# Feed-forward up projection with seven half-block products in place of eight, and its weights' low halves all made on VectorE

## The chip, the cores and the metric

The kernel runs on one core of one Trainium2 chip. The metric is the device time of one execution in microseconds. The kernel before takes 1625.59 us (median of 3 runs, 1625.49 to 1627.17).

## What is computed

Three blocks run one after another on a sequence of 512 tokens with 1024 features, in float32: a gated attention block, a gated retention block, and a mixer block (long convolution and gated linear attention) that ends in a feed-forward network. The change lies in that feed-forward network alone, which is the last stage before the final norm:

```python
def _sq_relu_mlp(h, w1, w2):
    return jnp.square(jax.nn.relu(h @ w1)) @ w2

        h2 = _rms_norm(x, norm_mlp[l]) * (1.0 + sc2) + sh2
        x = x + g2 * _sq_relu_mlp(h2, w_mlp1[l], w_mlp2[l])
    ...
    return _rms_norm(x, norm_final)
```

`h2` is 512 x 1024, `w1` 1024 x 4096, `w2` 4096 x 1024.

## The kernel before

Activations lie with features on the partitions: `X`, `HH` and `HL` are 128 x 8 x 512 (eight groups of 128 features, 512 tokens). Every float32 product is made from two halves: a value is split into a high half (rounded to fp32r) and a low half (the rest), and three matmuls are summed in PSUM: high x high, low x high, high x low. `HH` and `HL` are the high and low halves of the normed input, `FHI` and `FLO` those of the squared hidden activations.

Weights come as a stream of 246 tiles of 128 x 1024 values (512 KB), in the order of `PLAN`. Each tile is 512 input features by 256 output features. It is loaded into one of five `raw` buffers, ScalarE copies its high half into one of three `wh` buffers, and VectorE or GpSimd (the set `DVE_LOW` says which) subtracts to get the low half into one of three `wl` buffers. The class `Feed` sets where in each engine's program this is done: whenever an engine's code takes tile u, it first issues the work that it has on the tiles up to u + 2. Each engine works its program strictly in the order in which the code was written, so an instruction that waits holds up everything behind it.

An "up" unit u (0 to 15) makes 256 of the 4096 hidden features: two weight tiles, 48 matmuls of 512 columns (2 tiles x 2 output groups x 4 input groups x 3), in banks 0 and 1. Then ScalarE applies the relu out of PSUM, VectorE squares, ScalarE makes `FHI` (128 x 512), and VectorE or GpSimd makes `FLO`. A "down" unit takes a tile of `w2` in two output groups of 128 (nt = 0 in bank 0, nt = 1 in bank 1), with eight matmuls on the high half of the tile and four on the low half for each group; VectorE then adds the bank, scaled, to `X`. In the code `done("kept", tag, j)` is the mark that the bank j of a unit has been read, `free[b]` is what TensorE waits for before it starts a new sum in bank b, and `done("w free", u)` is the mark that TensorE has read tile u. Before the change the order is: up units in groups of four, then the four down units of the group before, each of these of two tiles (1024 hidden features).

TensorE instructions carry line 427 (all matmuls), ScalarE copies line 1972 (`copy`), other ScalarE work line 1969, VectorE's scalar_tensor_tensor line 1130. Both engines' code of the feed-forward part is in the functions `up` and `down`.

Of the kernel before, what the change touches and what calls it, by code (L numbers as in the profile page):

```python
# [19 lines left out]
T = 512  # L20
# [18 lines left out]

def weight_plan():  # L40
# [71 lines left out]
    down(3)
# [5 lines left out]
DVE_LOW = frozenset([*range(73), 164])  # L118
# [131 lines left out]
def build(nc, a, out, stack):  # L250
# [172 lines left out]
    def tensor(pe):  # L423
# [653 lines left out]
        unit_f(("up", 0, 0), (0, 1), *hi_lo("x3"), hooks=[nothing, first_scale, nothing, nothing])  # L1077

        def up(g):
            for n in range(4):  # L1080
                u = 4 * g + n
                if u:
                    unit_f(("up", g, n), (2, 3) if u == 1 else (0, 1), *hi_lo("x4"), by_k=2 if u == 1 else 0)

        def down(g):
            for n in range(4):
                for kh in range(2):
                    u = feed.take()
                    pe.wait_ge(*(done("l", "f", g, k) for k in range(4 * kh, 4 * kh + 4)))
                    features(("down", g, n), FHI[g % 2], FLO[g % 2], range(4 * kh, 4 * kh + 4), kh == 0, kh == 1, (0, 1), u,  # L1090
                             kh=kh)
# [31 lines left out]
    def vector(dve):  # L1123
# [18 lines left out]
        def split(i, u):  # L1142
            if u in DVE_LOW:
# [3 lines left out]
                by_dve.also("raw free", i)  # L1147

# [1827 lines left out]
```

## Time and profile before

| | |
|---|---|
| median of 3 runs | 1625.59 us |
| the profiled execution | 1626.04 us |
| its span | 1624.3 us |
| TensorE busy | 1607.9 us (99%) |
| TensorE weight load busy | 1336.6 us (82%) |
| VectorE busy | 829.1 us (51%) |
| ScalarE busy | 680.8 us (42%) |
| GpSimd busy | 583.0 us (36%) |
| DMA, mean | 110 GB/s |

Span is the time from the first to the last instruction in the trace; 1.7 us of the execution lie around it. Matmuls are pipelined, so the busy time of one matmul is longer than the distance from its start to the next one's start; the distance is what a matmul costs in a dense stretch.

### The profile page before, as it was taken

Reading aid. Unit: us, or ns where it says so; the run is one execution under the profiler, and the core shown is the slowest. Engines: PE = TensorE matmul, PEld = TensorE weight load, DVE = VectorE, ACT = ScalarE, POOL = GpSimd, SP = SyncE. Lnnn points to the kernel's source line nnn. Section 1 sums busy time; section 2 is a strip of 40 time slices with the busy share of each in tenths; the row PEclk is TensorE's granted clock in tenths of the full one; section 3 lists DMA queues with packets and bytes.
Section 4 is the critical chain, followed back from the end, with each engine's and each line's share of the span. In section 5 each row is a group of like instructions: output and inputs, shape, how many; then the busy total and the mean of one; then the engine's idle time right before and its main releaser. Section 6 shows DMA issues by size and latency. Waiting matters only on the chain.

```text
span 1624.3 us, 20270 instructions
## 1 busy us (share of the span) xinstructions
PE 1607.9 (99%) x8308; PEld 1336.6 (82%) x8308; DVE 829.1 (51%) x1239; ACT 680.8 (42%) x1043; POOL 583.0 (36%) x289
## 2 busy tenths in 40 slices
PE   9999999999999999999999999999999999999998
PEld 6888898889888878888887767789878788888887
DVE  7787867676665364443443646681356621111112
ACT  6533343443432433555455463423435643332323
POOL 1002113221344434334333434353323465555542
PEclk9999999999999999999999999999999999999999
DMA  6453333343355223233223241122112133222221
GB/s 234 153 204 131 125 127 134 116 132 121 133 205 207 104 91 104 93 103 103 94 90 121 78 156 66 52 87 73 53 40 78 65 117 104 91 103 92 98 85 52
DMA packets 53252, 179.16 MB, mean 110 GB/s; under 512 B 6428, under 2 KB 7068, under 8 KB 52776
## 3 DMA queue, kind: packets, MB, share of 16 engines
q1 hardware_dynamic: 53160, 177.88, 31.5%
q8 instruction: 65, 1.06, 0.3%
q14 instruction: 27, 0.22, 0.0%
HBM read 172.58 MB, written 2.12 MB: 108 GB/s over the span
## 4 chain that ended last, share of the span: by engine, by line
PE 92%; DVE 5%; ACT 1%; issue 1%; DMA 0%; SPq 0%; POOL 0%; DVEq 0%; ACTq 0%; POOLq 0%
PE banks L427 90%; PE banks L430 2%; DVE ACC L1182 1%; DVE wl L1146 1%; ACT T L1969 0%; DMA maskf<-cst_dram 0%; DVE ada L1130 0%; DVE X L1130 0%; ACT wh L1972 0%; ACT Sc L1969 0%; DVE ML L1130 0%; DVE T L1912 0%; ACT L1969 0%; DVE Sc L1130 0%; DVE E L1912 0%
## 5 line engine op out<-in xcount | busy, mean ns | idle before, releaser
L2553 POOL TENSOR_TENSOR wl<-raw,wh 128x1024 fp32r<-128x1024 f32 x171 | 424.2, 2485 | 525.3 <-ACT wh L1972 525.3
L427 PE MATMUL banks<-HH,wh 128*128 128x512 f32 (+1 forms) x1040 | 413.2, 397 | 2.6 <-ACT T L1969 0.9
L427 PE MATMUL banks<-HL,wh 128*128 128x512 f32 (+1 forms) x1040 | 402.3, 390 | 0.3 <-DVE HL L1130 0.3
L1972 ACT ACTIVATE wh<-raw 128x1024 fp32r<-128x1024 f32 x246 | 257.0, 1052 | 296.9 <-PE banks L427 289.0
L427 PE MATMUL banks<-HH,wl 128*128 128x512 f32 x1032 | 282.6, 390 | 0.0
L427 PEld LDWEIGHTS banks<-HH,wh 128*128 128x128 f32 (+1 forms) x1040 | 194.9, 187 | 50.0 <-issue 5.5
L427 PEld LDWEIGHTS banks<-HL,wh 128*128 128x128 f32 (+1 forms) x1040 | 194.7, 187 | 42.0 <-issue 1.4
L427 PEld LDWEIGHTS banks<-HH,wl 128*128 128x128 f32 x1032 | 193.4, 188 | 41.5 <-issue 1.0
L427 PE MATMUL banks<-wh,HH 128*128 128x256 f32 x448 | 128.5, 287 | 0.0
L427 PE MATMUL banks<-wl,HH 128*128 128x256 f32 x448 | 126.7, 283 | 0.0
L427 PE MATMUL banks<-wh,HL 128*128 128x256 f32 x448 | 126.6, 283 | 0.0
L1146 DVE TENSOR_TENSOR wl<-raw,wh 128x1024 fp32r<-128x1024 f32 x74 | 89.5, 1231 | 28.3 <-ACT wh L1972 28.3
L427 PE MATMUL banks<-OH,wh 128*128 128x512 f32 x256 | 103.1, 403 | 0.3 <-issue 0.3
L1130 DVE SCALAR_TENSOR_TENSOR X<-banks,mod,X 128x512 f32<-128x512 f32 (+1 forms) x41 | 30.1, 736 | 142.3 <-PE banks L427 142.3
L427 PE MATMUL banks<-OL,wh 128*128 128x512 f32 x256 | 99.8, 390 | 0.0
L427 PE MATMUL banks<-FHI,wh 128*128 128x512 f32 x256 | 99.6, 389 | 0.0
L427 PE MATMUL banks<-FLO,wh 128*128 128x512 f32 x256 | 99.6, 389 | 0.0
L2562 POOL TENSOR_TENSOR OL<-T,OH 128x512 fp32r<-128x512 f32 x21 | 28.3, 1349 | 197.4 <-ACT OH L1972 197.4
L1912 DVE TENSOR_TENSOR T<-T 128x512 f32<-128x512 f32 x30 | 28.3, 942 | 113.9 <-ACT T L1969 113.8
L427 PEld LDWEIGHTS banks<-wh,HL 128*128 128x128 f32 x448 | 85.7, 191 | 0.5 <-issue 0.2
L427 PEld LDWEIGHTS banks<-wh,HH 128*128 128x128 f32 x448 | 85.7, 191 | 0.5 <-issue 0.2
L427 PEld LDWEIGHTS banks<-wl,HH 128*128 128x128 f32 x448 | 85.7, 191 | 0.0
(354 smaller groups left out, 2627.5 us busy)
## 6 DMA issues: line engine op xcount, KB each, us to landing
raw<-wst_dram SPq DMA_DIRECT2D x294, 512.0 KB, 3.2
X<-xT_dram SPq DMA_DIRECT2D x8, 512.0 KB, 6.6
CB<-sums_dram SPq DMA_DIRECT2D x12, 256.0 KB, 3.1
D<-dec_dram SPq DMA_DIRECT2D x12, 256.0 KB, 2.8
out_dram<-XT SPq DMA_DIRECT2D x8, 256.0 KB
QS<-QX SPq DMA_DIRECT2D x24, 64.0 KB, 2.6
KSw<-KX SPq DMA_DIRECT2D x24, 64.0 KB, 2.0
MX<-memT_dram SPq DMA_DIRECT2D x2, 512.0 KB, 8.7
```

Of the source, the lines that this page charges most:

```text
L427: return pe.eng.matmul(dst, w, x, start=start, stop=stop, skip_group_check=True)
L430: return pe.eng.transpose(dst, x, ident[:, :])
L1130: return eng.scalar_tensor_tensor(out=dst, in0=x, scalar=s, in1=y, op0=op0, op1=op1)
L1146: tt(wl[:, q, :], raw[:, i % NRAW, :], wh[:, q, :].bitcast(F32), ALU.subtract).then_inc(*by_dve("low", u))
L1182: i = tt(acc[:, 0:n], acc[:, 0:n], q[:, 0:n], ALU.add)
L1912: tt(t[:, :], t[:, :], t[:, :], ALU.mult).then_inc(*by_dve("f", g, k))
L1972: return eng.activation(dst, src, ACT.Copy)
L2553: tt(wl[:, q, :], raw[:, i % NRAW, :], wh[:, q, :].bitcast(F32), ALU.subtract).then_inc(*by_pool("low", u))
L2562: tt(OL[:, tile, :], t[:, :], OH[:, tile, :].bitcast(F32), ALU.subtract).then_inc(*by_pool("l", "o", l, tile))
```

## The change

The up units 4 to 15 are computed by the Winograd form of Strassen's product. The weight tile is a 2 x 2 arrangement of blocks (256 input features by 128 output features each), the input a 2 x 2 arrangement (256 features by 256 tokens), and the product is made of seven block products in place of eight. Per tile these are seven products of 2 x 3 matmuls of 256 columns, 84 in a unit of two tiles, in banks 2 to 5. In place of each plain block some products take sums of blocks:

- of the weights: four sums per tile (`WS`), made on VectorE by three instructions (512, 256 and 256 elements), split by ScalarE (`SH`) and VectorE (`SL`)
- of the input: four sums per half (`XS`), made once in the units 2 and 3 on VectorE from `XW`, the whole values, which GpSimd adds from `HH` and `HL`; their halves are `XSH` and `XSL`
- of the products: ScalarE copies the first (`PS`), VectorE adds the others up by four instructions, and then makes relu and square in one instruction.

The order of the units changes too: each up unit from 2 on is followed by two down units of one tile each (512 hidden features), so that `FHI` and `FLO` hold half as many features and `X` is updated 64 times in place of 32. The set `DVE_LOW` now holds the tiles 192 to 245, so GpSimd makes no weights' low halves there (the tiles 190 and 191 are its last). GpSimd makes all `FLO` from unit 4 on.

```diff
+FF = [("up", 0), ("up", 1)]
+for _g in range(1, 8):
+    for _h in range(2):
+        FF += [("up", 2 * _g + _h), ("down", _g - 1, 2 * _h), ("down", _g - 1, 2 * _h + 1)]
+FF += [("down", 7, _n) for _n in range(4)]
...
+SEVEN = 4
...
+    for step in FF:
+        if step[0] == "up":
+            pair("up", 0, 8, (256 * step[1],), "s" if step[1] >= SEVEN else "w")
+        else:
+            pair("down", 4 * step[1], 4 * step[1] + 4, (256 * step[2],))
...
-DVE_LOW = frozenset([*range(73), 164])
+S_TILES = [u for u, w in enumerate(w for w in PLAN if w[0] != "ada") if w[0] == "s"]
+S_AT = {u: v for v, u in enumerate(S_TILES)}
+NS = 3
+DVE_LOW = frozenset([*range(73), 164, *range(192, 246)])
...
+        def seven(u):
+            for kh in range(2):
+                w = feed.take()
+                high, low = blocks(wh[:, w % NW, :]), blocks(wl[:, w % NW, :])
+                sums = [s[:, S_AT[w] % NS, :].rearrange("p (s q c) -> p s q c", s=4, q=2) for s in (SH_, SL_)]
+                def of_w(j, i):
+                    return high[:, j, :, i, :], low[:, j, :, i, :]
+                def of_s(n):
+                    return sums[0][:, n, :, :], sums[1][:, n, :, :]
+                def of_x(j, h):
+                    return [x[:, 4 * kh + 2 * j:4 * kh + 2 * j + 2, 256 * h:256 * h + 256] for x in (HH, HL)]
+                def of_t(n):
+                    return XSH[:, kh, n, :, :], XSL[:, kh, n, :, :]
+                def product(b, c, a, x):
+                    o, s0 = bank[b][:, 256 * c:256 * c + 256], kh == 0 and c == 0
+                    for q in range(2):
+                        mm(o, a[0][:, q, :], x[0][:, q, :], s0 and q == 0, False)
+                        mm(o, a[0][:, q, :], x[1][:, q, :], False, False)
+                    for q in range(2):
+                        i = mm(o, a[1][:, q, :], x[0][:, q, :], False, kh == 1 and q == 1)
+                    return i
+                pe.wait_ge(done("high", w), done("low", w), done("x sums", kh), *free[2])
+                product(2, 0, of_w(1, 0), of_x(1, 0))
+                product(2, 1, of_w(0, 0), of_x(0, 0)).then_inc(*by_pe("seven", u, kh, 0))
+                pe.wait_ge(done("sums high", w), done("sums low", w), *free[3])
+                product(3, 0, of_w(1, 1), of_t(3))
+                product(3, 1, of_s(2), of_t(1)).then_inc(*by_pe("seven", u, kh, 1))
+                pe.wait_ge(*free[4])
+                product(4, 0, of_s(1), of_t(0))
+                product(4, 1, of_s(0), of_t(2)).then_inc(*by_pe("seven", u, kh, 2))
+                pe.wait_ge(*free[5])
+                product(5, 0, of_s(3), of_x(1, 1)).then_inc(*by_pe("seven", u, kh, 3))
+                by_pe.also("w free", w)
...
+            for b in range(2, 6):
+                free[b] = tuple(done("kept", ("up", u), j) for j in range(2))
...
+        def down(g, n):
+            u = feed.take()
+            pe.wait_ge(*(done("l", "f", g, k) for k in range(4)))
+            features(("down", g, n), FHI[g % 2], FLO[g % 2], range(4), True, True, (0, 1), u)
...
+            if PLAN[i][0] == "s":
+                v = S_AT[u]
+                w, s = blocks(raw[:, i % NRAW, :]), WS[:, v % 2, :].rearrange("p (s q c) -> p s q c", s=4, q=2)
+                dve.wait_ge(done("raw", i), done("sums low", S_TILES[v - 2]) if v > 1 else done("l", "f", 0, 1))
+                tt(s[:, 0:2, :, :], w[:, 0, :, :, :].rearrange("p q i c -> p i q c"), w[:, :, :, 1, :],
+                   ALU.subtract).then_inc(*by_dve())
+                dve.wait_ge(by_dve.last())
+                tt(s[:, 2, :, :], w[:, 1, :, 1, :], s[:, 0, :, :], ALU.add).then_inc(*by_dve())
+                dve.wait_ge(by_dve.last())
+                tt(s[:, 3, :, :], w[:, 1, :, 0, :], s[:, 2, :, :], ALU.subtract).then_inc(*by_dve("summed", i))
+                dve.wait_ge(done("sums high", u))
+                tt(SL_[:, v % NS, :], WS[:, v % 2, :], SH_[:, v % NS, :].bitcast(F32), ALU.subtract).then_inc(*by_dve("sums low", u))
...
+        def x_sums(kh):
+            x = XW[:, 4 * kh:4 * kh + 4, :].rearrange("p (j q) (h c) -> p j q h c", q=2, c=256)
+            b11, b12, b21, b22 = (x[:, j, :, h, :] for j in range(2) for h in range(2))
+            dve.wait_ge(*(done("x whole", k) for k in range(4 * kh, 4 * kh + 4)), done("l", "f", 0, 1),
+                        done("x sums", kh - 1) if kh else None)
+            tt(XS[0][:, 0, :, :], b12, b11, ALU.subtract).then_inc(*by_dve())
+            stt(XS[1][:, 0, :, :], b22, -1.0, b12, ALU.mult, ALU.subtract).then_inc(*by_dve())
+            dve.wait_ge(by_dve.last())
+            tt(XS[0][:, 1, :, :], b22, XS[0][:, 0, :, :], ALU.add).then_inc(*by_dve("x summed", kh, 0))
+            dve.wait_ge(by_dve.last())
+            tt(XS[1][:, 1, :, :], b21, XS[0][:, 1, :, :], ALU.subtract).then_inc(*by_dve("x summed", kh, 1))
...
+        def seven(u):
+            g, n = u // 2, 2 * (u % 2)
+            kept = done("kept", ("up", u - 1), 0) if u > SEVEN else None
+            dve.wait_ge(done("seven", u, 1, 1), done("first product", u), kept)
+            tt(PS[:, 1, :], bank[3][:, 256:512], PS[:, 0, :], ALU.add).then_inc(*by_dve())
+            dve.wait_ge(done("seven", u, 1, 2), by_dve.last())
+            tt(PS[:, 2:4, :], psum[:, 4, :].rearrange("p (a c) -> p a c", a=2), PS[:, 1:2, :].to_broadcast([128, 2, 256]),
+               ALU.add).then_inc(*by_dve())
+            t = turn("hidden", g, n + 1)
+            dve.wait_ge(by_dve.last(), temp_free("hidden", g, n + 1))
+            tt(t[:, :].rearrange("p (a c) -> p a c", a=2), psum[:, 3:5, 0:256], PS[:, 3:4, :].to_broadcast([128, 2, 256]),
+               ALU.add).then_inc(*by_dve("kept", ("up", u), 1))
+            hidden(g, n + 1, t)
+            t = turn("hidden", g, n)
+            dve.wait_ge(done("seven", u, 1, 3), temp_free("hidden", g, n))
+            tt(t[:, :].rearrange("p (a c) -> p a c", a=2), psum[:, 2:6:3, 0:256], PS[:, 0:3:2, :],
+               ALU.add).then_inc(*by_dve("kept", ("up", u), 0))
+            hidden(g, n, t)
+        def hidden(g, k, t):
+            dve.wait_ge(by_dve.last())
+            stt(t[:, :], t[:, :], 0.0, t[:, :], ALU.max, ALU.mult).then_inc(*by_dve("f", g, k))
...
+            if u == 2:
+                x_sums(0)
+            if u == 3:
+                x_sums_low(1)
...
+        def down(g, n):
+            feed.take()
+            for j in range(2):
+                t = 2 * n + j
+                dve.wait_ge(done("unit", ("down", g, n), j), done("kept", ("down", g - 1, n), j) if g else None)
...
+                stt(X[:, t, :], bank[j], mod[:, 40 + t:41 + t], X[:, t, :], ALU.mult, ALU.add).then_inc(*by_dve("kept", ("down", g, n), j))
...
+            if (g, n) == (0, 0):
+                x_sums_low(0)
+            if (g, n) == (0, 1):
+                x_sums(1)
...
+            if PLAN[i][0] == "s":
+                v = S_AT[u]
+                act.wait_ge(done("summed", i), done("w free", S_TILES[v - NS]) if v >= NS else None)
+                copy(SH_[:, v % NS, :], WS[:, v % 2, :]).then_inc(*by_act("sums high", u))
...
+            if u >= SEVEN:
+                act.wait_ge(done("seven", u, 1, 0), done("kept", ("up", u - 1), 0) if u > SEVEN else done("x sums", 1))
+                copy(PS[:, 0, :], bank[2][:, 256:512]).then_inc(*by_act("first product", u))
+                for k in (2 * (u % 2) + 1, 2 * (u % 2)):
+                    high(g, k, temp("hidden", g, k))
...
-            if made[0] % 3:
+            if made[0] % 3 or g >= SEVEN // 2:
...
+        def x_whole(k):
+            pool.wait_ge(done("h", "x4", k), done("l", "x4", k))
+            tt(XW[:, k, :], HH[:, k, :].bitcast(F32), HL[:, k, :].bitcast(F32), ALU.add).then_inc(*by_pool("x whole", k))
...
+            for k in (1, 0) if u >= SEVEN else (0, 1):
+                k += 2 * (u % 2)
+                if low(g, k, temp("hidden", g, k)):
+                    by_pool.also("temp", turns["hidden", g, k])
+            if u == 1:
+                for j in range(2):
+                    low(g, j, E[j])
+            if u in (1, 2):
+                for k in range(4 * u - 4, 4 * u):
+                    x_whole(k)
```

VectorE, from the down units that stand before the up unit 4 on; a row "wl<-raw,wh" is the low half of a weight tile, "T<-T" is a square. Before, all of VectorE's work between the hidden features of two groups:

```order
L1912 TENSOR_TENSOR T_84<-T_84 128x512 [waits scalar_done]
L1130 SCALAR_TENSOR_TENSOR X<-banks,mod,X 128x512 [waits tensor_done] x8
L1912 TENSOR_TENSOR T_84<-T_84 128x512 [waits scalar_done]
L1912 TENSOR_TENSOR T_85<-T_85 128x512 [waits scalar_done]
L1916 TENSOR_TENSOR FLO_207<-T_85,FHI_205 128x512 [waits scalar_done]
```

And now, behind the low halves of the two down tiles that follow an up unit, to the first of these two tiles' update of `X`:

```order
L2010 TENSOR_TENSOR PS<-banks,PS 128x256 [waits scalar_done,tensor_done]
L2012 TENSOR_TENSOR PS<-banks,PS 128x512 [waits vector_done,tensor_done]
L2016 TENSOR_TENSOR T_84<-banks,PS 128x512 [waits gpsimd_done,vector_done]
L1186 SCALAR_TENSOR_TENSOR T_84<-T_84 128x512 [waits vector_done]
L2021 TENSOR_TENSOR T_85<-banks,PS 128x512 [waits gpsimd_done,tensor_done]
L1186 SCALAR_TENSOR_TENSOR T_85<-T_85 128x512 [waits vector_done]
L1202 TENSOR_TENSOR wl<-raw,wh 128x1024 [waits scalar_done]
L1208 TENSOR_TENSOR WS<-raw 128x512 [waits raw_in1]
L1211 TENSOR_TENSOR WS<-raw,WS 128x256 [waits vector_done]
L1213 TENSOR_TENSOR WS<-raw,WS 128x256 [waits vector_done]
L1215 TENSOR_TENSOR SL<-WS,SH 128x1024 [waits scalar_done]
L1186 SCALAR_TENSOR_TENSOR X<-banks,mod,X 128x512 [waits tensor_done] x2
```

Six instructions on the products and five on the next up unit's first tile now stand ahead of the update of `X` by the first down tile; nothing stood ahead of the eight updates before.

ScalarE at the same place, now (a row "wh<-raw" is the high half of a tile; the third of them is that of the next up unit's first tile):

```order
L2088 ACTIVATE wh<-raw 128x1024 [waits tensor_done,raw_in4]
L2088 ACTIVATE wh<-raw 128x1024 [waits tensor_done,raw_in0]
L2088 ACTIVATE PS<-banks 128x256 [waits tensor_done]
L2088 ACTIVATE FHI_214<-T_84 128x512 [waits vector_done]
L2088 ACTIVATE FHI_214<-T_85 128x512 [waits vector_done]
L2088 ACTIVATE wh<-raw 128x1024 [waits tensor_done,raw_in1]
L2088 ACTIVATE SH<-WS 128x1024 [waits vector_done]
```

The high half of the next up unit's first tile stands behind the two `FHI` of the unit before, which wait for VectorE.

TensorE, at the boundary between the two down tiles behind such an up unit, now (the last matmuls of the first tile, and the first of the second, which starts a new sum in bank 0):

```order
L445 MATMUL banks<-FHI_214,wh 128x512
L445 MATMUL banks<-FLO_216,wh 128x512
L445 MATMUL banks<-FHI_214,wl 128x512 x4
L445 MATMUL banks<-FHI_214,wh 128x512 [waits vector_done,scalar_done]
L445 MATMUL banks<-FLO_216,wh 128x512
```

The wait for `vector_done` is that for the first down tile's update of `X` out of bank 0 (`free[0]`).

GpSimd around the units 1 and 2, before:

```order
L2685 TENSOR_TENSOR FLO_207<-T_85,FHI_205 128x512 [waits vector_done,scalar_done]
L2685 TENSOR_TENSOR FLO_207<-E_204,FHI_205 128x512 [waits vector_done,scalar_done]
L2553 TENSOR_TENSOR wl<-raw,wh 128x1024 [waits scalar_done] x2
L2685 TENSOR_TENSOR FLO_207<-T_84,FHI_205 128x512 [waits vector_done,scalar_done]
L2553 TENSOR_TENSOR wl<-raw,wh 128x1024 [waits scalar_done] x2
```

And now:

```order
L2815 TENSOR_TENSOR FLO_216<-E_204,FHI_214 128x512 [waits vector_done,scalar_done]
L2820 TENSOR_TENSOR XW<-HH,HL 128x512 x4
L2683 TENSOR_TENSOR wl<-raw,wh 128x1024 [waits scalar_done] x2
L2815 TENSOR_TENSOR FLO_217<-T_84,FHI_215 128x512 [waits vector_done,scalar_done]
L2820 TENSOR_TENSOR XW<-HH,HL 128x512 x4
L2683 TENSOR_TENSOR wl<-raw,wh 128x1024 [waits scalar_done] x2
```

Four additions `XW` stand ahead of the low halves of the tiles 188 and 189, and four more ahead of those of 190 and 191.

## Rows read from the trace of the kernel before

**Rows 1.** The page: busy time by engine, and the chain that ended last

```profile
PE 1607.9 (99%) x8308; PEld 1336.6 (82%) x8308; DVE 829.1 (51%) x1239; ACT 680.8 (42%) x1043; POOL 583.0 (36%) x289
PE 92%; DVE 5%; ACT 1%; issue 1%; DMA 0%; SPq 0%; POOL 0%; DVEq 0%; ACTq 0%; POOLq 0%
```

**Rows 2.** Windows: the start, and the feed-forward stage from unit 3 on

```profile
0.00:8.00 8.00, 6.75 (x19) 2.54 (x19) 2.06 (x5) 3.68 (x4) 0.20 (x4) 1.00 0.76 250
1297.50:1614.00 316.50, 316.50 (x1399) 261.95 (x1399) 59.93 (x76) 101.35 (x127) 162.76 (x77) 1.00 0.25 88
```

**Rows 3.** Timeline of TensorE: matmuls of 512 columns, 12 from 1371.32 to 1374.04

```profile
1371.32 0.39 PE L427 MATMUL banks<-FHI,wh 128*128 128x512 f32 x1
...
1374.04 0.39 PE L427 MATMUL banks<-FHI,wh 128*128 128x512 f32 x1
```

**Rows 4.** Timeline of TensorE: matmuls of 256 columns, 55 from 269.87 to 276.47

```profile
269.87 0.28 PE L427 MATMUL banks<-wh,HH 128*128 128x256 f32 x1
...
276.47 0.28 PE L427 MATMUL banks<-wh,HL 128*128 128x256 f32 x1
```

**Rows 5.** Timelines of VectorE and ScalarE: what TensorE's progress releases

```profile
1371.52 0.75 DVE L1130 SCALAR_TENSOR_TENSOR X<-banks,mod,X 128x512 f32<-128x512 f32 x1 [7.41 <-PE banks L427]
...
1374.30 1.06 ACT L1972 ACTIVATE wh<-raw 128x1024 fp32r<-128x1024 f32 x1 [4.38 <-PE banks L427]
```

**Rows 6.** Groups by shape: durations on ScalarE, VectorE and GpSimd

```profile
L1972 ACT ACTIVATE FHI<-T 128x512 fp32r<-128x512 f32 x30 | 19.0, 633 | 30.3 <-DVE T L1912 30.3
L1969 ACT ACTIVATE T<-banks 128x512 f32<-128x512 f32 x35 | 20.8, 595 | 44.8 <-PE banks L427 44.7
L1904 DVE TENSOR_TENSOR E<-banks,R 128x512 f32<-128x512 f32 x2 | 1.3, 680 | 0.0
L1368 DVE TENSOR_TENSOR PL<-banks,PH 128x256 fp32r<-128x256 f32 x12 | 5.0, 413 | 0.0
L1130 DVE SCALAR_TENSOR_TENSOR HL<-X,gx,HH 128x512 fp32r<-128x512 f32 x8 | 6.0, 747 | 1.5 <-ACT HH L1969 1.5
L1146 DVE TENSOR_TENSOR wl<-raw,wh x74: 1208/1217/1714, 6.3 to 1074.2; 128x1024 fp32r<-128x1024 f32 x74
L1916 DVE TENSOR_TENSOR FLO<-T,FHI x9: 692/692/1007, 1302.8 to 1517.7; 128x512 fp32r<-128x512 f32 x9
```

**Rows 7.** The chain, in order of time: from VectorE's end to TensorE's start

```profile
1196.17 0.77 DVE KEC L1760 x2
1196.94 0.14 issue
1197.08 0.94 PE banks L427 x3
```

**Rows 8.** Timelines of GpSimd and VectorE around 1301 to 1311 us

```profile
1301.47 1.75 POOL L2685 TENSOR_TENSOR FLO<-T,FHI 128x512 fp32r<-128x512 f32 x1
1303.75 4.75 POOL L2553 TENSOR_TENSOR wl<-raw,wh 128x1024 fp32r<-128x1024 f32 x2 [0.54 <-ACT wh L1972]
1309.79 1.29 POOL L2685 TENSOR_TENSOR FLO<-T,FHI 128x512 fp32r<-128x512 f32 x1 [1.29 <-ACT FHI L1972]
...
1300.43 1.63 DVE L1912 TENSOR_TENSOR T<-T 128x512 f32<-128x512 f32 x1 [1.18 <-ACT T L1969]
...
1306.87 2.18 DVE L1912 TENSOR_TENSOR T<-T 128x512 f32<-128x512 f32 x1 [3.11 <-ACT T L1969]
1310.23 1.40 DVE L1912 TENSOR_TENSOR T<-T 128x512 f32<-128x512 f32 x1 [1.18 <-ACT T L1969]
```

**Rows 9.** Timelines of GpSimd and TensorE around the end of unit 2

```profile
1295.06 1.30 POOL L2685 TENSOR_TENSOR FLO<-E,FHI 128x512 fp32r<-128x512 f32 x1 [1.89 <-ACT FHI L1972]
1296.31 5.21 POOL L2553 TENSOR_TENSOR wl<-raw,wh 128x1024 fp32r<-128x1024 f32 x2
...
1297.51 0.47 PE L427 MATMUL banks<-HH,wh 128*128 128x512 f32 x1 [0.94 <-ACT T L1969]
```

**Rows 10.** TensorE: its first matmuls, and its longest waits in the whole trace

```profile
1.25 7.03 PE L427 MATMUL banks<-Z 128*128 128x512 bf16 x18 [1.25 <-DVE Z L1263]
PE banks L427 <- DVE wl L1146: 2.3, 4, 1.0
```

More of the change, by code:

```diff
@@ L1075, in first_scale @@
             free[6] = (done("sum kept", "x3"),)
[L1077 to L1091, printed above, removed]
@@ L1894, in norm_half @@
             for k in ks:
-                dve.wait_ge(done("scale rows", "x3"), done("l", "x4", k - 2) if k > 1 else None, *(done("half", ("up", 0, 0), kh, j) for j in range(2)))
+                dve.wait_ge(done("scale rows", "x3"), done("l", "x4", k - 2) if k > 1 else None, *(done("half", ("up", 0), kh, j) for j in range(2)))
                 stt(bank[4 + k % 2], X[:, k, :], gx2[:, k:k + 1], bank[7], ALU.mult, ALU.mult).then_inc(*by_dve("x4", k))
@@ new lines, in x_sums_low @@
+        def x_sums_low(kh):
+            for n in range(2):
+                dve.wait_ge(done("x sums high", kh, n), done("x summed", kh, 1))
+                tt(XSL[:, kh, 2 * n:2 * n + 2, :, :], XS[n][:, :, :, :], XSH[:, kh, 2 * n:2 * n + 2, :, :].bitcast(F32),
+                   ALU.subtract).then_inc(*by_dve("x sums", kh))
+        def seven(u):
[16 more added lines that the diff above has]
+            hidden(g, n, t)
@@ new lines, in down @@
+        def down(g, n):
[3 more added lines that the diff above has]
+                dve.wait_ge(done("unit", ("down", g, n), j), done("kept", ("down", g - 1, n), j) if g else None)
+                if g == 7 and t == 7:
+                    for h in range(2):
+                        c = slice(256 * h, 256 * h + 256)
+                        stt(X[:, t, c], bank[j][:, c], mod[:, 40 + t:41 + t], X[:, t, c], ALU.mult, ALU.add).then_inc(*by_dve("last tile", h))
+                    by_dve.also("kept", ("down", g, n), j)
+                    turn("last", "x5")
+                    continue
+                stt(X[:, t, :], bank[j], mod[:, 40 + t:41 + t], X[:, t, :], ALU.mult, ALU.add).then_inc(*by_dve("kept", ("down", g, n), j))
+                if g == 7:
+                    add_square("x5", t, T, t == 0, t == 6, free=done("sum", "x3"))
+            if (g, n) == (0, 0):
+                x_sums_low(0)
+            if (g, n) == (0, 1):
+                x_sums(1)
@@ L1955, in vector @@
+        for step in FF[1:]:
+            (up if step[0] == "up" else down)(*step[1:])
         dve.wait_ge(done("root"))
@@ new lines, in down @@
+        def down(g, n):
+            if (g, n) == (7, 0):
+                fn(sm[:, 0:1], one, ACT.Sqrt).then_inc(*by_act())
+            feed.take()
+            for j in range(2):
+                t, m = 2 * n + j, done("kept", ("down", g, n), j)
+                if g == 7 and t == 7:
+                    q = temp("last", "x5")
+                    act.wait_ge(temp_free("last", "x5"))
+                    for h in range(2):
+                        c = slice(256 * h, 256 * h + 256)
+                        act.wait_ge(done("last tile", h))
+                        fn(q[:, c], X[:, t, c], ACT.Square).then_inc(*by_act("last square half", h))
+                elif g == 7:
+                    square("x5", t, X[:, t, :], T, m)
+                if g == 7:
+                    act.wait_ge(m, done("seven", 15, 1, 3))
+                    fn(XG[:, t, :], X[:, t, :], ACT.Copy, scale=P("gfin", t)).then_inc(*by_act("weighted", t))
+            if (g, n) == (0, 1):
+                x_sums_high(1)
@@ L2531, in scalar @@
+        for step in FF[1:]:
+            (up if step[0] == "up" else down)(*step[1:])
         act.wait_ge(done("sum col", "x5"))
```

180 lines of the change are left out of this document (67 added, 113 removed).

## Prediction

> **What bounds the kernel now.** I read the page first. TensorE is busy 99% of the span, and 92% of the chain that ended last is TensorE [rows 1]. The windows then say whether the changed stage is like the whole: from 1297.5 to 1614 us TensorE is busy for all of 316.5 us, at a granted clock of 1.00, while VectorE has 59.9 us of work, ScalarE 101.4 and GpSimd 162.8 [rows 2]. So the stage costs what its matmuls cost, and three engines have slack in total. Whether the slack lies where the change needs it is a question of order, not of sums. The list of waits says that TensorE's longest waits are short: the largest entry is 2.3 us in four waits [rows 10].
>
> What does a matmul cost? Not its busy time but its distance to the next. Twelve matmuls of 512 columns go from 1371.32 to 1374.04: 0.2267 us each [rows 3]. Fifty-five of 256 columns go from 269.87 to 276.47: 0.1200 us each, not half of 0.2267 (0.1133) [rows 4].
>
> **The saving on TensorE.** A unit now is 48 x 0.2267 = 10.88 us; with seven products it is 84 x 0.1200 = 10.08 us. Seven eighths would give 9.52; more than half of the saving goes into the shorter matmuls. 12 units x 0.80 = **-9.6 us**. The down units keep their matmuls (24 per tile, 5.44 us).
>
> The Trainium skill (TensorE: Matmul & The Clock Gate, "Back-to-back issue gap") gives a distance of N/2.4 GHz + 2.5 ns: 215.8 and 109.2 ns. By it the saving would be 12 x (10.36 - 9.17) = 14.2 us in place of 9.6, an estimate from that page. The trace disagrees by some 11 ns per matmul at either size, so the rows decide.
>
> **The new wait, walked once.** Let t = 0 be when TensorE begins the first down tile behind an up unit. It needs 5.44 us for it; then the second down tile starts a new sum in bank 0, which must have been read by the first tile's update of `X`. That update stands on VectorE behind six instructions on the products and five on the next up unit's first tile (the order of the change). VectorE sees a mark 0.20 us after TensorE would start its next matmul (1371.52 against 1371.32 [rows 3, 5]), ScalarE after 0.26.
>
> - Product six ends at -0.72, seen at -0.52. Three sums out of PSUM and two squares: 0.68 each for sums, 0.75 for squares [rows 6]. Order: sum to 0.16, sum to 0.84, square to 1.59, sum to 2.27, square to 3.02. (The first, of 256, is done before that.)
> - ScalarE: second `FHI` 0.63 to 3.65; only then the high half of the next tile, 1.06 [rows 5], to 4.7. Its own data and buffer were free at 0.
> - VectorE: low half 1.21, to 5.9. Weight sums 0.69 + 0.41 + 0.41 (nearest rows: 512 elements with two SBUF inputs, 256 elements [rows 6]) to 7.4. ScalarE splits them, 1.06 (the same copy), to 8.5. VectorE's low half of the sums, 1.21, to 9.7. The update of `X`, 0.75 to 10.45; TensorE starts 0.14 later [rows 7], at 10.6.
>
> TensorE waits 10.6 - 5.44 = 5.15 us, if nobody disturbs VectorE. But GpSimd makes two `FLO` here, 1.29 each, the first from 2.3 on. The timelines price the overlap [rows 8]: VectorE squares of 512 elements with both inputs in SBUF take 1.40 to 2.18 us beside GpSimd (0.69 alone is the nearest in kind [rows 6]), and each ends some 0.55 after GpSimd's: 1308.50 and 1309.05, 11.08 and 11.63. GpSimd's `FLO` beside a square takes 1.75 in place of 1.29. One waits for the other. If the second square goes first, the `FLO` run from 3.05 to 5.65 and the low half of the tile ends at 5.65 + 1.1 = 6.75 in place of 5.9: the wait is 6.0. If GpSimd goes first, the square ends at 3.6 + 0.55, the high half at 5.85, the second `FLO` at 6.15, the low half at 7.25: 6.5. The two are ready within 0.1 us of each other; I take 6.0, and keep 5.15 and 6.5 as bounds.
>
> Does it get worse or better further on? In the second down tile the same five instructions stand ahead of its update, but no `FHI`; VectorE goes through them from 12 to 17.5, while TensorE, now late, ends that tile at 17 and next works the up unit in banks 2 to 5, for 10 us, with all it needs ready. So the debt is paid off and each round begins alike. Behind the units 4 to 14 that is 11 waits: 11 x 6.0 = **+66 us** (57 to 71).
>
> Behind unit 3 the same, with relu (0.60 [rows 6]), square, `FHI` and two low halves of the input sums (1.2 each) ahead of the tile: 0.26 + 0.60 + 0.69 + 2.4 + 1.2 + 1.5 + 1.06 + 1.2 + 0.75 + 0.14 = 9.8, a wait of 4.4, or 7.0 if two `FLO` get in the way. I take **+6**. Behind unit 15 the next tile needs no sums: high half to 4.7, low half to 6.75, update 7.5, start 7.65, a wait of **+2.2** (1.4 undisturbed). The last tiles need only 1.2 us of low half in 5.44 and wait for nothing.
>
> **The early part.** GpSimd began the low half of tile 188 at 1296.31, and TensorE began its unit at 1297.51 [rows 9]. Four `XW` additions, at 1.3 us each like an `FLO`, now stand ahead of it: it is ready at 1296.31 + 5.2 + 2.6 = 1304.1. TensorE wants it after eight matmuls, at 1299.3: a wait of 4.8. On VectorE four input sums stand ahead of the update of `X` by the first down tile. They can start at 1301.5; if each has a GpSimd instruction ahead of it (2.4, 2.4, 1.3, 1.3), they end at 1301.5 + 7.4 + 2.8 = 1311.7, and the second down tile starts at 1312.6 and not at 1307.75. That is up to 4.9 more. I take **+9** for both (4.8 to 9.7). The `XW` ahead of tiles 190 and 191 find GpSimd with two down tiles' time, 10.9 us, for 5.2 + 4.8.
>
> **At no cost:** 32 more updates of `X`, 32 x 0.75 = 24 us on an engine with 256 us of slack, outside the walk; the two operations that VectorE does in one for relu and square; loads, since the raw tiles are the same 64 and the DMA share is 0.25 [rows 2]. GpSimd loses 52 or so low halves of 2.4 us; nobody waited for them, so that gives nothing.
>
> Sum: -9.6 + 66 + 6 + 2.2 + 9 = +73.6 us on the profiled execution of 1626.0 (span 1624.3), which is 0.45 above the median: 1699.2. With all lower bounds -9.6 + 56.7 + 4.4 + 1.4 + 4.8 = +57.7, 1683; with all upper ones -9.6 + 71.5 + 7.0 + 2.2 + 9.7 = +80.8, 1706. **Forecast 1699 us.**
>
> **Rivals.**
>
> *TensorE's clock falls in the waits.* Nothing before shows an idle time of 5 us in TensorE, so the 1.00 of [rows 2] is no evidence for after. The nearest row is the start: 18 matmuls of 512 columns take 7.03 us [rows 10], so 17 distances in 6.64, where 17 x 0.2267 = 3.85 is the later pace: 2.8 us lost after an idle engine. If all 12 long waits end so, +34: 1733; if half, 1716. The Trainium skill (same page, "HAM oscillation — how this bites in real kernels") has idle stretches between bursts of matmuls put the clock back to its lower level; it speaks for this rival. I give it 0.30 (1707 to 1740).
>
> *The walk is too long.* Waits of 3 to 5 us: VectorE's and ScalarE's instructions overlap their starts, as two low halves in a row do before, and `FLO` falls into gaps. 11 x 4 + 4 + 1 + 5 - 9.6 = +44: 1670. Each term above is the time of an instruction alone, so some of this is real. 0.14 (1650 to 1683).
>
> *Not slower.* The saving stands and the updates of `X` come in time. That needs the time from the last products to the update to be under 5.44 us, where my walk has 10.6; it would be so if the weight sums (1.5 + 1.06 + 1.2) and half of the rest were off this path. Only the early wait would be left: 1626 - 9.6 + 4.8 = 1621. The share of busy time speaks for it (VectorE would be busy some 18 us of each 27), the order of the instructions against. 0.03; another 0.01 for landing within 0.2%, which is about what a measurement of this kernel can tell from no change.
>
> *Worse than all that*, over 1740, by early waits that grow: 0.02. My forecast, 1683 to 1707, has 0.50.
>
> The range 1677 to 1732 leaves out about 2 in 10. Slower by over 0.2%: 0.96; within: 0.01; faster: 0.03.
>
> **What the profile after would show.** The distance of the 256-column matmuls should be 0.120 us, in up units of 10.1 us. TensorE should have 11 idle times of some 6 us, all ahead of the second down tile of a round, released by VectorE's update of `X`; a round should last 21.0 + 6.0 = 27.0 us, against 21.8 for the same tiles before. VectorE's five instructions on the weight tile should end right before that update. One wait of about 5 us should lie in the first down tile, released by GpSimd's low half. I am wrong if TensorE's second down tile starts without idle time, if the idle times are released by something else (`SL` or a raw load), or if the spacing of matmuls right behind a wait is 0.2 us for 256 columns or 0.4 for 512, which would be the clock.

## The result

The changed kernel takes 1724.23 us (median of 4 runs, 1723.76 to 1726.18); the kernel before, run beside it, 1625.73 us. The ratio is 1.0606, 95% interval 1.0588 to 1.0625: 6% slower. The profiled execution took 1723.76 us, with a span of 1722.0 us. 1699 was forecast, in a range of 1677 to 1732; the time lies in the case in which TensorE's clock falls in the waits (1707 to 1740, chance 0.30).

The page of the changed kernel: busy time by engine, the granted clock in 40 slices, and the chain that ended last.

```profile
PE 1628.9 (95%) x8740; PEld 1367.9 (79%) x8740; DVE 1028.3 (60%) x1473; ACT 698.7 (41%) x1059; POOL 484.4 (28%) x251
...
PEclk9999999999999999999999999999999898989899
...
PE 81%; DVE 12%; ACT 4%; issue 2%; DMA 0%; POOL 0%; SPq 0%; DVEq 0%; ACTq 0%; POOLq 0%
```

Against [rows 1], TensorE is 95% busy and no longer 99%, and VectorE has gone from 5% to 12% of the chain. The digits of the clock fall to 8 in every other slice at the end: something regular.

The waits of TensorE in the changed kernel from 1240 to 1722 us, by what ended them (total, times, longest):

```profile
PE banks L445 <- DVE X L1186: 70.4, 14, 6.6
PE banks L445 <- POOL wl L2683: 5.4, 1, 5.4
PE banks L445 <- ACT T L2085: 1.9, 2, 1.0
```

Nothing in [rows 10] is of that size. One round, on the timeline of TensorE:

```profile
1543.17 0.76 PE L445 MATMUL banks<-FHI,wh 128*128 128x512 f32 x1 [5.49 <-DVE X L1186]
1543.73 0.63 PE L445 MATMUL banks<-FLO,wh 128*128 128x512 f32 x1
1544.16 0.63 PE L445 MATMUL banks<-FHI,wh 128*128 128x512 f32 x1
...
1547.73 0.39 PE L445 MATMUL banks<-FHI,wh 128*128 128x512 f32 x1
1547.95 0.39 PE L445 MATMUL banks<-FLO,wh 128*128 128x512 f32 x1
...
1550.45 0.28 PE L445 MATMUL banks<-HH,wh 128*128 128x256 f32 x1
...
1560.52 0.40 PE L445 MATMUL banks<-FHI,wh 128*128 128x512 f32 x1
...
1571.63 0.76 PE L445 MATMUL banks<-FHI,wh 128*128 128x512 f32 x1 [5.49 <-DVE X L1186]
```

The up unit takes 1560.52 - 1550.45 = 10.07 us for 84 matmuls, 0.1199 each, as forecast. The first down tile should end 5.44 later, at 1565.96; the second starts at 1571.63: a wait of 5.67. And the matmuls right behind a wait are 0.43 us apart and not 0.2267. The windows of the same stretch (columns as in [rows 2]; the granted clock follows the five engines) name it:

```profile
1537.00:1543.10 6.10, 0.68 (x4) 0.22 (x2) 4.91 (x7) 2.00 (x2) 0.41 (x1) 0.75 0.25 86
1543.10:1545.00 1.90, 1.83 (x4) 1.49 (x5) 1.90 (x3) 0.00 (x0) 0.00 (x0) 0.50 0.00 0
1545.00:1547.00 2.00, 2.00 (x6) 1.59 (x5) 1.26 (x3) 0.64 (x1) 0.00 (x0) 0.53 0.00 0
1547.00:1549.00 2.00, 2.00 (x10) 1.64 (x9) 1.54 (x2) 0.42 (x1) 0.00 (x0) 1.00 0.68 262
```

In the wait the clock is already down in part (0.75), then 0.50, that is 1.2 GHz, and then 1.00 again. The next round differs in where the clock falls:

```profile
1566.00:1571.60 5.60, 0.15 (x1) 0.00 (x0) 4.41 (x7) 2.00 (x2) 0.00 (x0) 0.93 0.27 94
1575.00:1577.00 2.00, 2.00 (x6) 1.52 (x6) 1.08 (x1) 0.89 (x1) 0.00 (x0) 0.50 0.50 156
```

Worked out from the granted clock of these windows (0.75 over 6.10 us, 0.93 over 5.60 us), the lower clock covers some 3 us of the first wait but only 0.8 us of the second; in the second round it still holds at 1577, 5.4 us into the work. So the matmuls of the first lose 1.9 us and those of the second 2.9 us, for the same wait.

All of the loss can be counted on the timeline: for each matmul the distance to the next one's start, less 0.2267 or 0.1200. From 1285 us to the last down unit, the excess at waits is 79.4 us (before: 1.1), the excess elsewhere, which is the slow matmuls behind waits, 29.2 us (before: 0.3). 78.3 + 28.9 - 9.6 (the saving) = 97.6; the spans differ by 1722.0 - 1624.3 = 97.7. So these terms account for the difference, to about 1 us: counted on every matmul of the trace and not on the rows of the timeline, the excess elsewhere is 30.1.

What VectorE, ScalarE and GpSimd do from the last products to the update of `X`, on their timelines:

```profile
1560.00 0.69 DVE L2012 TENSOR_TENSOR PS<-banks,PS 128x512 f32<-128x512 f32 x1 [1.02 <-PE banks L445]
...
1562.78 0.69 DVE L1186 SCALAR_TENSOR_TENSOR T<-T 128x512 f32<-128x512 f32 x1
1565.12 1.84 DVE L1202 TENSOR_TENSOR wl<-raw,wh 128x1024 fp32r<-128x1024 f32 x1 [1.65 <-ACT wh L2088]
1566.88 0.68 DVE L1208 TENSOR_TENSOR WS<-raw 128x512 f32<-128x512 f32 x1
...
1569.60 1.22 DVE L1215 TENSOR_TENSOR SL<-WS,SH 128x1024 fp32r<-128x1024 f32 x1 [1.12 <-ACT SH L2088]
1570.74 1.40 DVE L1186 SCALAR_TENSOR_TENSOR X<-banks,mod,X 128x512 f32<-128x512 f32 x2
...
1563.50 0.63 ACT L2088 ACTIVATE FHI<-T 128x512 fp32r<-128x512 f32 x1 [0.69 <-DVE T L1186]
1564.04 1.04 ACT L2088 ACTIVATE wh<-raw 128x1024 fp32r<-128x1024 f32 x1
...
1562.89 2.99 POOL L2815 TENSOR_TENSOR FLO<-T,FHI 128x512 fp32r<-128x512 f32 x2 [25.48 <-ACT FHI L2088]
```

With zero at the end of the up unit (1560.52) the squares end at 2.95 (walk: 3.02), the high half at 4.56 (4.7), the low half beside GpSimd's `FLO` at 6.44 (6.75), the sums at 8.0, their high half at 9.1, and the update begins at 10.2. Of the 11.0 us to the end of the first update VectorE stands idle for 1.65 + 1.12.

Early, on GpSimd's timeline, the four `XW` take 5.87 us, and the low half of tile 188 comes so late that TensorE waits 5.42 us in the first down tile:

```profile
1295.65 5.87 POOL L2820 TENSOR_TENSOR XW<-HH,HL 128x512 f32<-128x512 f32 x4
1301.47 5.57 POOL L2683 TENSOR_TENSOR wl<-raw,wh 128x1024 fp32r<-128x1024 f32 x2
```

### The profile page after: what moved, and what is told of

It is laid out like the page before. It is cut to its first block, busy times and chain, and to the rows that moved or that the text cites. A ratio compares the mean times of both kernels' runs of the same rounds, so it can differ in the third digit from the quotient of the medians.

```text
span 1722.0 us, 21475 instructions
## 1 busy us (share of the span) xinstructions
PE 1628.9 (95%) x8740; PEld 1367.9 (79%) x8740; DVE 1028.3 (60%) x1473; ACT 698.7 (41%) x1059; POOL 484.4 (28%) x251
## 4 chain that ended last, share of the span: by engine, by line
PE 81%; DVE 12%; ACT 4%; issue 2%; DMA 0%; POOL 0%; SPq 0%; DVEq 0%; ACTq 0%; POOLq 0%
PE banks L445 80%; DVE wl L1202 2%; PE banks L448 2%; ACT wh L2088 1%; DVE ACC L1250 1%; DVE X L1186 1%; DVE SL L1215 1%; ACT SH L2088 1%; DVE T L1186 1%; DVE PS L2012 0%; DVE T L2016 0%; DVE T L2021 0%; DMA maskf<-cst_dram 0%; ACT T L2085 0%; DVE WS L1208 0%
## 5 line engine op out<-in xcount | busy, mean ns | idle before, releaser
L2683 POOL TENSOR_TENSOR wl<-raw,wh 128x1024 fp32r<-128x1024 f32 x117 | 296.4, 2540 | 418.2 <-ACT wh L2088 418.2
L445 PE MATMUL banks<-HH,wh 128*128 128x512 f32 (+2 forms) x944 | 363.2, 387 | 2.4 <-ACT PH L2088 0.8
L445 PE MATMUL banks<-HL,wh 128*128 128x512 f32 (+2 forms) x944 | 352.7, 379 | 0.4 <-DVE HL L1186 0.4
L445 PE MATMUL banks<-HH,wl 128*128 128x512 f32 (+1 forms) x936 | 250.5, 379 | 0.0
L1202 DVE TENSOR_TENSOR wl<-raw,wh 128x1024 fp32r<-128x1024 f32 x128 | 164.1, 1295 | 101.3 <-ACT wh L2088 101.3
L445 PEld LDWEIGHTS banks<-HH,wh 128*128 128x128 f32 (+1 forms) x944 | 177.2, 188 | 42.5 <-issue 5.9
L445 PEld LDWEIGHTS banks<-HL,wh 128*128 128x128 f32 (+1 forms) x944 | 177.0, 188 | 35.2 <-issue 1.4
L445 PEld LDWEIGHTS banks<-HH,wl 128*128 128x128 f32 x936 | 172.3, 188 | 33.9 <-issue 1.0
L2815 POOL TENSOR_TENSOR FLO<-T,FHI 128x512 fp32r<-128x512 f32 x29 | 43.9, 1530 | 321.5 <-ACT FHI L2088 321.5
L445 PEld LDWEIGHTS banks<-FHI,wh 128*128 128x128 f32 x256 | 56.1, 219 | 89.3 <-issue 66.1
```

The source lines that it names most:

```text
L445: return pe.eng.matmul(dst, w, x, start=start, stop=stop, skip_group_check=True)
L1202: tt(wl[:, q, :], raw[:, i % NRAW, :], wh[:, q, :].bitcast(F32), ALU.subtract).then_inc(*by_dve("low", u))
L2683: tt(wl[:, q, :], raw[:, i % NRAW, :], wh[:, q, :].bitcast(F32), ALU.subtract).then_inc(*by_pool("low", u))
L2815: tt(FLO[g % 2][:, k, :], t[:, :], FHI[g % 2][:, k, :].bitcast(F32), ALU.subtract).then_inc(*by_pool("l", "f", g, k))
```

## Experiments

All are compared with the kernel before on the same chip. "Theory A" is that the whole loss is the waits behind VectorE's queue and the lower clock that follows them.

**1. The updates of `X` first.** In VectorE's `down` the call that works on the next weight tile goes behind the two updates:

```diff
         def down(g, n):
-            feed.take()
+            if g == 7:
+                feed.take()
             for j in range(2):
                 ...
                 stt(X[:, t, :], bank[j], mod[:, 40 + t:41 + t], X[:, t, :], ...)
+            if g < 7:
+                feed.take()
```

> Edit: VectorE's two updates of X by a down tile stand ahead of its work on the weight tile that is split in that step; nothing else changes. Theory A (the loss is the wait for the first down tile's update of X behind VectorE's weight work, 11 waits of 5.65 us, and the lower clock that follows each, some 2.3 us a round): by the same walk the update is done at 3.75 us of the 5.44 us that cover it, so the 11 waits and the clock loss go. The early waits stay (5.6, 1.9 and up to some us behind unit 3), and VectorE may now be late with the sums of the second tile by 0.6 us a round: 1625 to 1640 us. Rival B (the seven products as such cost it: shorter matmuls, more loads, more work on VectorE in total): the order of VectorE's work matters little, above 1700 us.

Measured: 1634.03 us, ratio 1.0052 (1.0037 to 1.0067), clock 0.999. Moving one call gives back 90 of 98 us. TensorE's waits in this run, from 1285 to 1625 us:

```profile
PE banks L445 <- POOL wl L2686: 5.4, 1, 5.4
PE banks L445 <- DVE SL L1215: 3.9, 11, 0.4
PE banks L445 <- DVE X L1186: 3.7, 2, 2.1
PE banks L445 <- ACT T L2088: 1.0, 1, 1.0
```

And its timeline, at the second tile of an up unit:

```profile
1542.62 0.36 PE L445 MATMUL banks<-XSH,wh 128*128 128x256 f32 x1 [0.36 <-DVE SL L1215]
```

The eleven waits for `X` are gone; what is next late is `SL`, the low half of the second tile's sums, by 0.52 us in distance (0.36 by the row), where 0.6 was expected. Rival B falls: the same seven products, the same 256-column matmuls and the same work on VectorE are all here.

**2. TensorE kept at work in the waits.** The second down tile of a pair gets extra matmuls ahead of it, in bank 6, whose results nobody reads:

```diff
+            if n % 2 and (g, n) not in ((0, 1), (6, 3)) and g < 7:
+                for r in range(23):
+                    mm(bank[6], FHI[g % 2][:, r % 4, 0:128], FHI[g % 2][:, r % 4, :], True, True)
             features(("down", g, n), FHI[g % 2], FLO[g % 2], range(4), True, True, (0, 1), u)
```

> Edit: 23 extra matmuls of 512 columns (5.2 us) into the unused bank 6 ahead of the second down tile behind the units 3 to 14, their results unused. Theory A: they lie inside the waits of 5.65 us, which stay as they are; the granted clock stays at 1.00 there, and the 12 stretches of slower matmuls (about 26 of the 29 us lost to the clock) go: about 1698 us. Rival C (the matmuls behind a wait are slower for another reason, such as cold buffers, and the clock column only follows): no gain, 1724 us or more.

Measured: 1697.90 us, ratio 1.0444 (1.0429 to 1.0460). The windows of the stage in this run:

```profile
1345.00:1690.00 345.00, 340.27 (x1982) 299.36 (x1980) 217.89 (x280) 107.09 (x131) 35.86 (x24) 1.00 0.22 71
```

The granted clock is 1.00, where the changed kernel has 0.90 from 1340.7 to 1710 us, a round is 26.76 us (1475.21 to 1501.97) and not 28.95, and 26.3 us come back though 276 matmuls were added. So the slow stretches are the clock's, and it is TensorE's idleness that lets it fall. Rival C falls. The time is what was expected (1698).

**3. GpSimd makes the low halves.** This undoes the half of the change that the title names second:

```diff
-DVE_LOW = frozenset([*range(73), 164, *range(192, 246)])
+DVE_LOW = frozenset([*range(73), 164])
```

> Edit: GpSimd makes the low halves of the tiles 192 to 245 again, as before; the seven products stay. Theory A: the low half (1.84 us beside GpSimd's FLO) leaves VectorE's queue ahead of the update of X, the sums can start when the squares end, and VectorE idles less: the walk gives an update at 7.7 us, a wait of some 2.5 us in place of 5.65, and a wait of 2.5 us may leave the clock alone: 1660 to 1690 us. If GpSimd's 2.4 us beside VectorE's two-input instructions block as much as they save, it stays near 1720 us. Rival B: unchanged or slower.

Measured: 1731.01 us, ratio 1.0649 (1.0633 to 1.0664): not better but 7 us worse. The 1660 to 1690 us of the expectation missed it; its other branch, that GpSimd blocks as much as it saves (near 1720), comes closer and is still too low. The timelines of VectorE and GpSimd say why:

```profile
1540.93 1.78 DVE L1208 TENSOR_TENSOR WS<-raw 128x512 f32<-128x512 f32 x1
1542.75 1.40 DVE L1211 TENSOR_TENSOR WS<-raw,WS 128x256 f32<-128x256 f32 x1
1544.18 2.44 DVE L1213 TENSOR_TENSOR WS<-raw,WS 128x256 f32<-128x256 f32 x1
...
1540.43 3.43 POOL L2815 TENSOR_TENSOR FLO<-T,FHI 128x512 fp32r<-128x512 f32 x2 [3.62 <-ACT FHI L2088]
1543.82 2.52 POOL L2683 TENSOR_TENSOR wl<-raw,wh 128x1024 fp32r<-128x1024 f32 x1
```

The three weight sums take 0.68, 0.42 and 0.43 alone, and 1.78, 1.40 and 2.44 beside GpSimd: each has a GpSimd instruction in front of it. In all, 4.1 us of blocking take the place of a low half of 1.84 (the wait becomes 6.25, the one behind unit 3 9.07 in place of 6.79, and the one behind unit 15 is gone). VectorE's making of the low halves was thus not what cost; here it is the better of the two. The Trainium skill (SBUF — State Buffer, "Who interferes with whom") says that a VectorE instruction with two SBUF inputs contends with a GpSimd instruction that reads SBUF, and that the port pair they share is an exclusive lock. These rows agree: the second sum ends at 1544.15, 0.29 us behind the second `FLO`, and the third at 1546.62, 0.28 us behind the low half.

**4. Eight products in the new order.** `SEVEN = 16`, so no unit uses seven; the sums of the input are made and not used. ScalarE's wait for the end of unit 15 goes to the mark that this unit now has.

> Edit: no unit uses seven products (eight everywhere), but the new order of units and VectorE's low halves from tile 192 on stay, and so do the input sums, made and not used. Theory A: with no weight sums and no product sums ahead of it, the update of X stands at about 5.4 us, at the edge of its cover of 5.44 us; the early waits stay (7.5 us): 1633 to 1645 us. Rival D (the new order of the units and VectorE's low halves are what costs, not the sums): above 1690 us.

Measured: 1639.82 us, ratio 1.0089 (1.0072 to 1.0106). TensorE waits four times from 1285 to 1620 us:

```profile
PE banks L445 <- POOL wl L2683: 5.4, 1, 5.4
PE banks L445 <- DVE X L1186: 4.2, 2, 2.7
PE banks L445 <- ACT T L2085: 1.0, 1, 1.0
```

No round has a wait. The order of the units and VectorE's low halves fit into the 5.44 us; it is the sums ahead of the update that do not. This run is also 5.8 us slower than experiment 1, which has the seven products. Its longest wait for `X` (2.90 us in distance, behind unit 3) left the granted clock at 1.00. Rival D falls.

**5. ScalarE's high half ahead of `FHI`.** The chain itself is shortened, with VectorE's order as changed:

```diff
                 copy(PS[:, 0, :], bank[2][:, 256:512]).then_inc(*by_act("first product", u))
+                feed.take()
                 for k in (2 * (u % 2) + 1, 2 * (u % 2)):
                     high(g, k, temp("hidden", g, k))
...
         def down(g, n):
-            feed.take()
+            if n % 2 or g in (0, 7):
+                feed.take()
```

> Edit to the changed kernel: ScalarE makes the high half of the next up unit's first tile (and the high half of its sums) ahead of the two FHI of the unit that ends, not behind them. Theory A (the walk: the wait is the length of a chain, in which VectorE stands idle 1.65 us for this high half and 0.6 us for GpSimd's FLO): VectorE's low half starts when its squares end, at 3.0 us in place of 4.6, and FLO moves behind the sums, so the update of X is done some 2.3 us earlier: waits of 3.4 us in place of 5.65. That is 11 x 2.3 = 25 us less; if waits of 3.4 us leave the clock at 1.00, another 25 us: 1675 to 1700 us. A rival (the chain is set by VectorE's total work, not by its idle time in it): 1720 us.

Measured: 1695.31 us, ratio 1.0433 (1.0417 to 1.0449). The waits are 3.29 us in distance (3.4 expected), so the walk holds step by step. The clock is spared in two rounds only (below). One wait and what follows on TensorE's timeline:

```profile
1549.34 0.47 PE L445 MATMUL banks<-FHI,wh 128*128 128x512 f32 x1 [3.13 <-ACT wh L2088]
1549.64 0.39 PE L445 MATMUL banks<-FLO,wh 128*128 128x512 f32 x1
...
1550.76 0.63 PE L445 MATMUL banks<-FLO,wh 128*128 128x512 f32 x1
```

And in the windows:

```profile
1546.00:1549.30 3.30, 0.21 (x1) 0.00 (x0) 2.18 (x4) 3.04 (x4) 1.43 (x1) 1.00 0.51 159
1549.30:1550.30 1.00, 0.96 (x4) 0.86 (x5) 1.00 (x2) 0.00 (x0) 1.00 (x2) 1.00 0.00 0
1550.30:1553.70 3.40, 3.40 (x9) 2.62 (x8) 3.15 (x4) 0.15 (x1) 0.61 (x1) 0.51 0.00 0
```

Here the clock falls 1 us after work has begun again. (The row puts the wait down to ScalarE's `wh`, which is of a later tile and which this matmul does not need; it ended at 1549.26, 0.07 us after the update of `X` that the matmul does need, and the matmul began 0.15 us after that update. A wait for several marks shows the last that came.) The excess of slow matmuls is 26.9 us in this run, for waits of 3.3 us, against 29.2 for waits of 5.65; both sums hold the same early waits (5.6 and 6.8 us), which cost 1.9 and 2.5 us here. The rounds are not alike. Behind the first two waits of 3.30 us the clock stays up (the first on the timeline, then the windows behind both):

```profile
1367.30 0.47 PE L445 MATMUL banks<-FHI,wh 128*128 128x512 f32 x1 [3.14 <-ACT wh L2088]
1367.30:1373.00 5.70, 5.70 (x26) 4.75 (x27) 4.50 (x6) 1.06 (x1) 1.57 (x2) 1.00 0.09 15
1391.60:1397.00 5.40, 5.34 (x24) 4.46 (x25) 4.20 (x6) 1.06 (x1) 1.64 (x2) 1.00 0.04 7
```

They lose 0.1 us each, and the other nine 1.4 to 3.0 us each, for the same wait. So a wait of 3.3 us makes the clock fall in most rounds and not in all, and this kernel's runs spread from 1693.81 to 1699.43 us.

**6. `FLO` out of the chain.**

```diff
+            if u >= SEVEN:
+                pool.wait_ge(done("kept", FF[FF.index(("up", u)) + 1], 0))
             for k in (1, 0) if u >= SEVEN else (0, 1):
```

> Edit to the changed kernel: from unit 4 on GpSimd makes the two FLO of a unit only after the first down tile's update of X, so they are out of the chain. Theory A with the term for contention: the low half of the tile takes 1.22 in place of 1.84 us, so each of 11 waits is 0.62 us shorter, 5.0 us, and the time 1717 us, the clock loss as before. If the time stays at 1724, the contention was not on the path; if it falls by more than 12 us, the clock is spared at 5.0 us.

Measured: 1712.08 us, ratio 1.0533 (1.0517 to 1.0548). The waits are 5.02 us, as expected: 11 x 0.62 = 6.9 us. The waits behind unit 15 and ahead of the second down tile of all (1.17 and 0.88) give 1.6 more, and the clock 3.1: the excess of slow matmuls is 26.1 in place of 29.2. The expectation (1717 us) left out both. It also took a fall of over 12 us as a sign that the clock is spared; the time fell by 12.15 us and the clock was not spared.

**7. Updates first in the first tile of a pair only.** As in 1, with `g == 7 or n % 2` in place of `g == 7`.

> Edit to the changed kernel: as in the run with the updates of X first, but only in the first down tile of each pair; in the second one VectorE's weight work stands first again. Theory A: the 11 waits of 0.52 us for the second tile's sums go too, and nothing takes their place, since bank 0 is next wanted after a whole up unit: 1634.0 - 5.7 = 1628 us, with the early waits of 9.6 us as the rest of the loss.

Measured: 1627.54 us, ratio 1.0015 (1.0005 to 1.0024). The waits for `SL` are gone and none took their place. What remains is early: 5.56, 1.79 and 1.78 us, with 2.5 us of slow matmuls behind the first.

**8. And the early work spread.** On top of experiment 7, seven products from unit 6 on, and:

```diff
-SEVEN = 4
+SEVEN = 6
-DVE_LOW = frozenset([*range(73), 164, *range(192, 246)])
+DVE_LOW = frozenset([*range(73), 164, *range(200, 246)])
...
-            if u in (1, 2):
-                for k in range(4 * u - 4, 4 * u):
-                    x_whole(k)
+            for k in {2: (0, 1), 3: (2, 3, 4), 4: (5, 6, 7)}.get(u, ()):
+                x_whole(k)
...
-            if (g, n) == (0, 0):
-                x_sums_low(0)
-            if (g, n) == (0, 1):
-                x_sums(1)
+            if (g, n) in ((0, 3), (1, 1)):
+                x_sums(g)
```

`x_sums_low` goes to the start of the units 4 and 5, `x_sums_high` beside `x_sums`.

> Edit: the run before this one, with the seven products from unit 6 on and not 4 (GpSimd keeps the low halves up to tile 199), the eight XW additions spread over the units 2 to 4, none ahead of unit 2's weights, and the input sums made behind the second tile of a pair. Theory A: the early waits of 9.6 us and their clock loss of 2 to 3 us go; two units lose their saving of 0.8 us each: 1628 - 9.6 - 2.5 + 1.6 = 1617.5 us, under the kernel before by some 8 us, which is 10 units x 0.8 us. A rival (GpSimd beside more VectorE work makes other early waits): 1622 to 1630 us.

Measured: 1618.70 us (1618.60 to 1619.78), ratio 0.9959 (0.9945 to 0.9974): 0.4% faster than the kernel before, beyond the interval. The windows from 1297.5 to 1600 us:

```profile
1297.50:1600.00 302.50, 301.48 (x1724) 266.15 (x1723) 212.11 (x275) 113.02 (x137) 74.34 (x45) 1.00 0.29 93
```

TensorE is as good as never idle there and the clock is 1.00, with VectorE at 212 us of work and not 59.9 [rows 2].

**9. The same with eight products.** `SEVEN = 16` in kernel 8, with ScalarE's wait as in experiment 4.

> Edit: the run before this one (updates of X first in the first tile of a pair, XW spread) with eight products in every unit; the order of the units, VectorE's low halves and the input sums, now unused, stay. Theory A: no wait of TensorE differs, so the two differ by the matmuls alone: 10 units x (10.88 - 10.08) = 8.0 us more than with seven, 1626.7 us, the time of the kernel before within 2 us. If the seven products cost something that the trace of the waits does not show, the difference is smaller than 8 us.

Measured: 1627.02 us, ratio 1.0010 (1.0001 to 1.0019). The difference to 8 is 8.3 us for 10 units, where 8.0 was worked out: the seven products are worth their 0.8 us a unit, no less. (The two ran on different chips; the kernel before took 1625.42 and 1625.41 us on them.)

## Why the prediction was right, and where not

The cause that was forecast is the cause that was found: the waits, their place and what ends them. The time, though, lies in the range only because the range took in part of the rival on the clock. The forecast's own bounds (1683 to 1706) do not reach it: +74 us was forecast and +98 measured.

- *The saving, -9.6 us*: right. 0.1199 us per matmul in the up units, and experiments 8 and 9 give 0.83 us a unit. The formula of the Trainium skill (TensorE: Matmul & The Clock Gate, "Back-to-back issue gap") would have given 1.19, an estimate from its figures. One sentence of the prediction misreads its own sum: seven eighths would save 1.36 us a unit, 0.80 is saved, so 0.56 (four tenths, not "more than half") goes into the shorter matmuls.
- *The wait behind the units 4 to 14, +66*: right in place, releaser and mechanism, a little large: 11 x 5.65 = 62.1. The clock apart, a round is 26.6 us and not 27.0. The term for GpSimd's `FLO` in it was taken as 0.85 us and is 0.62 (experiment 6).
- *Behind unit 3, +6*: 6.8. *Behind unit 15, +2.2*: 1.8. *Early, +9*: 7.5, of which 5.6 for the low half of tile 188 (4.8 worked out; the `XW` took 5.87 us and not 5.2, slowed by VectorE's squares) and 1.9 for the second down tile.
- *All waits together*: 83.2 forecast, 78.3 measured.
- *The step that failed is the choice between the forecast and the first rival*: "TensorE's clock falls in the waits" was given 0.30 and the clock's staying up 0.50. It falls at the long waits and costs 28.9 us. The trace before had no wait over 1.3 us in TensorE, and I took the lack of evidence as weight for the case without it. The price was fair: at 2.8 us for each of 12 waits, worked out from the start of the trace, it would have been 34, with half of them 17. The rival should have been the likeliest case: 1699 with 28.9 more, less 5 for the smaller waits, is 1723. What the Trainium skill says in "HAM oscillation — how this bites in real kernels" (same page), which I had cited against my own forecast, agrees with this trace: the clock is at 0.50 behind the waits of 5.65 us.
- *"Each round begins alike"*: right for the waits (5.65 in all eleven), not for the clock: rounds alternate between 28.5 and 29.5 us.
- *The other rivals*: "the walk is too long" was right by 5 us only. "Not slower" fell as forecast, but experiment 1 shows how near it lay: in the order of one call.

Two points stay open. The rounds lose 1.9 or 2.9 us to the clock according to how far ahead of the next matmul it falls; why it falls sooner in one wait than in the next, and why it stayed up behind two waits of 3.3 us, no run shows. And the three waits that were left in experiment 7 were removed in 8 together with a later start of the seven products, so how much of the 8.8 us each of these two edits brings is argued from the waits, not shown.

## What to carry to other kernels

An engine that is 60% busy, as VectorE is here behind the change, can still be the one that all wait for: what counts is how much stands in its queue between the event that releases it and the result that somebody needs, against the time that covers it (here 10.2 us against 5.4), so walk one round before adding work to a slack engine, and put the instruction that frees a PSUM bank ahead of work for later tiles where that bank is wanted soon (in the first down tile of a pair alone it gave back 97 us, experiment 7; in the second one too it cost 0.5 us a round, experiment 1). Price a wait of TensorE of the size seen here (3.3 to 6.8 us) with the slow matmuls behind it: 1.4 to 3.0 us each, but for two waits of 3.3 us that cost 0.1. Do so even where the trace at hand has no such wait. A saving of arithmetic that shortens the matmuls loses part of itself: seven eighths of the work took 93% of the time.

## What the runs showed that I had not expected

The clock fell behind nine of eleven waits of 3.3 us as well as behind all of 5.65 us, and cost nearly as much (26.9 against 29.2 us in all), so a shorter wait gave back little more than itself. In the wait of 3.3 us that is shown it fell only after the matmuls had begun again. Three VectorE sums of 1.5 us together took 5.6 us beside GpSimd, because each waited for another GpSimd instruction: three short two-input instructions lost 4.1 us there, one long one 0.6 (the low half, 1.84 in place of 1.22).
